# Second layer: separate SBUF places for the mixer weights of the second tile, and one load of each query weight for both tiles

## Chip, core and metric

The kernel runs on one core of a Trainium2 chip, as one launch. The metric is the time of that launch on the device, in microseconds, as the median of several runs. All data are float32; matrix products that feed later selections are formed either in float32 or as three float32r products (a high and a low part).

## What is computed

256 tokens of width 1024 go through two layers, 128 tokens (one tile) at a time where the text says tile 0 and tile 1. The first layer (a mixer, cross attention to a memory, and a layer of retrieved experts) is untouched by the change. The second layer, cut to what matters:

```python
n1 = rmsnorm_2(h, norm1_g)
proj = n1 @ w_in                       # q, k, v, r, a_lr, su, sv, ga, gb
y_a = gla_branch(...);  y_b = sgu_branch(...)
merged = sigmoid(ga) * (y_a @ w_branch_a) + sigmoid(gb) * (y_b @ w_branch_b)
h = h + merged @ w_out
n2 = rmsnorm_2(h, norm2_g)
h = h + peer_2(n2, peer_wq, ...)       # q = n2 @ peer_wq; scores against two key sets;
                                       # top 16 of 16 x 16 per head, 8 heads: 128 of 16384 experts per token
                                       # out = sum over the 128 of gate * gelu(u[e] . n2) * v[e]
return rmsnorm_2(h, final_g)
```

## The kernel before

**Weights.** Every large weight lies in HBM as chunks of 128 x 2048 float32 (1024 KB) in `wall`, and each chunk is one DMA, issued on the SP queue by `chunk` (L400) or `keep` (L412). The second layer's chunks go to a ring of four places, `WP` (columns 8192 to 16384 of the tile `BIG`, in the profile `big_sb`). `ring_w2.take(use, done)` hands out the next place and gives back the event that frees it: the read of the chunk that had the place four loads ago. SP waits for that event, then issues, and everything behind it in SP's program waits too.

**Uses.** For tile t the mixer of the second layer has four `up` chunks, ("up", 2, t, half, n), two for each branch, and four `square` chunks, ("sq", 2, t, n), the output projection. TensorE reads them at L863 (`up`) and L880 (`square`). Then come eight query chunks, one per head, ("q", 2, t, h), read at L966; the scores of two heads at a time are L981. Tile 0 takes heads 0 to 7 in order. Heads 4 to 7 of tile 0 go to places of their own, `KQ` (columns 24576 to 32768, where tile 1's gates and the constants of the mixer lie; so `keep` waits until tile 1's merge `mix_v "mg", 2, 1, 1` is over), and tile 1 starts with these four, as its uses 0 to 3. Its uses 4 to 7 are heads 0 to 3, which SP loads again through the ring. SP's list for the second layer is thus: 16 projection chunks, 4 `up` and 4 `square` of tile 0, heads 0 and 1, the `up` chunks of tile 1 with heads 2 and 3 between them, 4 `square` of tile 1, kept heads 4 to 7, and heads 0 to 3 once more (in `weights2`, L487 on).

**Experts.** Tile 0's first product with `u` is done by gathering: 128 indirect DMAs (L2317, GpSimd's own queue), each bringing one row of 1024 to each token (512 KB), into eight slots `UB`, columns 0 to 8192 of `BIG`. Two of three are multiplied and summed on VectorE (L2092), the third on GpSimd (L2338) and ScalarE. A slot is refilled when the dot product eight steps earlier is done. For tile 1 the product is dense: all 16384 rows of `u`, as 128 chunks `ut` of 512 KB on SP's queue (L581), four slots, read by TensorE at L1002; ScalarE takes every fourth chunk's results through gelu. In the same stretch one-hot gate blocks are formed on VectorE and multiplied on TensorE (L1021). Last come the values `v`: 128 chunks on SP's queue, read at L1040 and L1054.

**Order.** Each engine has one program. It is made of strands (generators), each of which yields a number, its beat, ahead of each piece, and `in_turn` merges the strands by these beats when the program is built. The beats are no times on the chip; they only fix an order, for each engine by itself. What runs when is settled by semaphores. VectorE's order around the change: `experts(2)`, the dot products, has beats from 1276 in steps of 2, tile 1's norm has 1278 to 1281; so the dot products of gathers 0 and 2 stand ahead of the two halves of tile 1's norm product. GpSimd's order is that of its gathers with a multiplication after each third. SP's order is the one given above, with `ut` chunks 0 to 3 at beat 1250 and the later ones from 1290 on, each behind the dense product four chunks before.

Around the change: `weight` (which place and which semaphore belong to a use), `weights2` (SP's order), `rows` of the GpSimd program (the gathers of `u`).

Of the kernel before, what the change touches and what calls it, by code (L numbers as in the profile page):

```python
# [13 lines left out]
WR = 4  # L14
UR = 8
FD = 640
RAW_COLS = 512
DR = 4
# [209 lines left out]
def build(nc, a):  # L228
    with ExitStack() as ctx:
# [10 lines left out]
        BIG = sb("big_sb", [128, 32768])  # L240
# [41 lines left out]
        def small(n, *name):  # L282
            if name not in columns:
# [60 lines left out]
        SQUARE = {1: 34, 2: 78, "co": 42}  # L344
# [11 lines left out]
             "gla_p gla_a gla_v gla_g sgu_p sgu_a sgu_v sgu_g kv_p kv_a").split()]  # L356
        vec_in, ident_in, wsm_in, cst_in, row_in, subk2_in, sguw_in, gup_in, wlr_in, sgub_in = loads = [landing(n) for n in (
            "vec_in ident_in wsm_in cst_in row_in subk2_in sguw_in gup_in wlr_in sgub_in").split()]
        x_in, mem_in, w_in, kq_in, tq_in, sub_in, u_in, ut_in, v_in, low_in, out_in = slots = [
            [landing(f"{n}{i}") for i in range(k)] for n, k in (  # L360
                ("x_in", 2), ("mem_in", 2), ("w_in", WR), ("kq_in", 4), ("tq_in", 4), ("sub_in", 6), ("u_in", UR), ("ut_in", DR), ("v_in", 6), ("low_in", 6), ("out", 2))]

        ring_a, ring_b, ring_c, ring_m = Ring(banks[2:4]), Ring(banks[4:6]), Ring(banks[6:8]), Ring(banks[0:2])
        WP = [BIG[:, 8192 + 2048 * i:8192 + 2048 * (i + 1)] for i in range(WR)]
# [4 lines left out]
        second = lambda use: use[0] in ("in2", "kv") or (use[0] in ("up", "sq", "q") and use[1] == 2)  # L369

        KQ = [BIG[:, 24576 + 2048 * i:24576 + 2048 * (i + 1)] for i in range(4)]
        TQ = [BIG[:, o:o + 2048] for o in (29696, 20992, 16384, 18432)]
        kept = lambda use: use[0:2] == ("q", 2) and (use[2] == 0 and use[3] > 3 or use[2] == 1 and use[3] < 4)

        def weight(use):
            if use in (("q", 1, 0, 4), ("q", 1, 0, 5), ("q", 1, 0, 6), ("q", 1, 0, 7), ("q", 1, 1, 1), ("q", 1, 1, 2), ("q", 1, 1, 3)):
                return TQ[use[3] % 4], tq_in[use[3] % 4].at("q")
            if kept(use):
                return KQ[use[3] % 4], kq_in[use[3] % 4].at(use[1])
            ring = ring_w2 if second(use) else ring_w  # L380
            return ring.place(use), w_in[ring.index(use)].at(use)
# [10 lines left out]
        def sync_program(e):  # L392

            def chunk(use, i, done):

                ring = ring_w2 if second(use) else ring_w
                place, free = ring.take(use, done)
                for f in free:
                    e.wait_ge(*f)
                e.dma_start(place, a["wall"][i]).then_inc(*w_in[ring.index(use)].up(use))  # L400
# [86 lines left out]
            def weights2():  # L487
                for n in range(4):
                    yield 860 + 32 * n
                    e.wait_ge(*val_v.at("gl", 1, STEPS.index((79 + 16 * n, (0, 1)))))  # L490
                    chunk(("kv", n), 54 + n, (kv_p, "kv", n, 1))
                for n in range(16):
                    yield 1085 + 3.4 * n if n < 4 else (1097, 1102, 1113, 1119, 1126, 1133, 1139, 1146, 1154, 1159, 1165, 1171)[n - 4]
                    chunk(("in2", n), 58 + n, (split_v, "lo", ("in2", n)))
                def up(t, h, n):
                    chunk(("up", 2, t, h, n), UP[2, h] + n, (mix_p, "up", 2, t, h, n))

                def square(t, n):
                    chunk(("sq", 2, t, n), SQUARE[2] + n, (mix_p, "sq", 2, t, n))

                def query(t, h):
                    if t == 0 and h > 3:
                        keep(2, h, mix_v.at("mg", 2, 1, 1))
                    else:
                        chunk(("q", 2, t, h), PQ[2] + h % 4, (sel_p, "q", 2, t, h))

                for h, n, b in ((0, 0, 1176), (0, 1, 1182), (1, 0, 1187), (1, 1, 1193)):
                    yield b
                    up(0, h, n)
                for n in range(4):  # L510
                    yield (1204, 1207, 1211, 1215)[n]
                    square(0, n)
                yield 1220
                query(0, 0)
                query(0, 1)
                for n in range(2):
                    yield 1228 + 5 * n
                    up(1, 0, n)
                    query(0, 2 + n)
                for n in range(2):  # L520
                    yield 1238 + 2 * n
                    up(1, 1, n)
                for n in range(4):
                    yield 1245 + 3 * n
                    square(1, n)
                for t, h in [(0, h) for h in range(4, 8)] + [(1, h) for h in range(4, 8)]:
                    yield 1264 + 0.1 * h if t == 0 else 1306 + 4 * h
                    query(t, h)

            def rows():  # L530
                yield 119.5
# [1746 lines left out]
        def gpsimd_program(e):  # L2278
# [40 lines left out]
            def rows(l):  # L2319
                T, dt = T_GATHER[l]  # L2320
                for k in range(128):
                    yield T + dt * k
                    if k % 32 == 0:
                        e.wait_ge(*sel_v.at("ix", l, 0, k // 32))
                    if k == 0:
                        e.wait_ge(*proj_p.at("mm", ("mv", 3) if l == 1 else ("in2", 15)))
                    if k >= UR:
                        e.wait_ge(*(dot_a if pooled(k - UR) else dot_v).at("dot", l, k - UR))
                    gather(UB[k % UR], a[f"u{l}"], k).then_inc(*u_in[k % UR].up(l, k))
# [137 lines left out]
```

## Time and profile before

| | |
|---|---|
| median of 3 runs | 2080.87 us (2074.07 to 2081.56) |
| the profiled execution | 2079.94 us, its span 2078.2 us |
| mean granted TensorE clock | 0.976 |
| busy, share of the span | TensorE 92%, weight loads of TensorE 81%, VectorE 66%, ScalarE 43%, GpSimd 38% |
| DMA | 627.08 MB, mean 302 GB/s |
| SP's queue (q1), software queue (q0), share of 16 DMA engines | 51.9%, 27.6% |
| weight loads on SP's queue | 123 issues into `big_sb`, 1024 KB each |

A row of a timeline gives the start and the length of a group of like instructions, the engine, the line, the operation with its tiles, how many they are, and in brackets the idle time of the engine before it with what ended it. SPq is the issuing of DMAs by SP, not their transfer. In the table by stage each row gives a stretch, its length, busy time of each engine with its instructions, the granted clock of TensorE, the busy share of the 16 DMA engines and what they moved. In rows on waits stand the total, how often, and the longest.

### The profile page before, as it was taken

The page shows a single profiled execution, that of the slowest core. Times are in us where ns is not written, and L with a number is a line of the kernel's source. Part 1 is how long each engine was busy: PE and PEld are TensorE (multiplying, and loading weights), DVE is VectorE, ACT ScalarE, POOL GpSimd, SP SyncE. Part 2 cuts the span into 40 slices and gives each one's busy share as a digit, 9 for nine tenths or more (in the row PEclk, how much of TensorE's full clock was granted, in tenths as well). Part 3 has the DMA queues.
Part 4 walks back from the last instruction along what each step waited for, and adds up shares of the span by engine and source line. Part 5 has one row for each costly group of instructions (what it writes and reads, how often), then busy time and mean ns, then how long its engine had stood idle before and what let it go on. Part 6 is the DMA issues. An engine that isn't in the chain of part 4 may idle for free.

```text
span 2078.2 us, 32948 instructions
## 1 busy us (share of the span) xinstructions
PE 1908.6 (92%) x12722; PEld 1673.2 (81%) x12722; DVE 1374.9 (66%) x2722; ACT 900.7 (43%) x1946; POOL 780.3 (38%) x626
## 2 busy tenths in 40 slices
PE   6999999987888999999999999887798899899998
PEld 6999988877888989676666889877798799767775
DVE  6643431378989948587775333268588798688884
ACT  5555443123236747444442553113223577544442
POOL 0000000068686635344431000047577744444441
PEclk9999999998999999999999999999999999999999
DMA  5433453899999988999995433699999978799996
GB/s 230 160 127 121 148 214 128 338 357 359 375 405 399 372 303 281 339 386 404 398 382 204 162 122 123 209 388 410 379 399 383 410 295 264 293 379 391 391 389 253
DMA packets 154874, 627.08 MB, mean 302 GB/s; under 512 B 19271, under 2 KB 22983, under 8 KB 138846
## 3 DMA queue, kind: packets, MB, share of 16 engines
q1 hardware_dynamic: 97374, 406.84, 51.9%
q0 software_dynamic: 57344, 218.14, 27.6%
q8 instruction: 101, 1.65, 0.3%
q14 instruction: 55, 0.45, 0.1%
HBM read 623.85 MB, written 1.05 MB: 301 GB/s over the span
## 4 chain that ended last, share of the span: by engine, by line
PE 35%; DMA 7%; issue 4%; DVE 2%; ACT 2%; POOL 0%; SPq 0%; DVEq 0%; POOLq 0%
PE bank L1002 7%; PE bank L1040 7%; PE bank L1054 5%; DMA ut_sb<-in_ut_dram 5%; PE bank_n L1054 4%; PE bank L966 3%; PE bank L1021 2%; PE bank L1085 1%; DMA big_sb<-in_u_dram,idx_sb 1%; PE bank L620 1%; PE bank L621 1%; PE bank L622 1%; DMA nt_sb<-in_v_dram 1%; PE bank L863 1%; DMA ab_sb<-in_v_dram 1%
## 5 line engine op out<-in xcount | busy, mean ns | idle before, releaser
L1002 PE MATMUL bank<-nt_sb,ut_sb 128*128 128x128 f32 x4096 | 508.4, 281 | 62.2 <-DMA ut_sb<-in_ut_dram 58.9
L1002 PEld LDWEIGHTS bank<-nt_sb,ut_sb 128*128 128x128 f32 x4096 | 486.2, 196 | 74.1 <-DMA ut_sb<-in_ut_dram 59.3
L2317 POOL DMA_INDIRECT big_sb<-in_u_dram,idx_sb x256 | 255.3, 997 | 243.7 <-ACT big_sb L1166 116.9
L1166 ACT ACTIVATE big_sb<-bank 128x512 f32<-128x512 f32 (+13 forms) x284 | 131.9, 477 | 352.5 <-PE bank L1002 127.7
L2281 POOL TENSOR_TENSOR sm_sb<-sm_sb,vec_sb 128x1 f32<-128x1 f32 (+2 forms) x24 | 19.5, 813 | 640.2 <-DVE sm_sb L1671 634.6
L2092 DVE CUSTOM_DVE_ANT_0 big_sb<-big_sb,bank_n 128x1024 f32<-128x1024 f32 x170 | 205.5, 1211 | 70.4 <-DMA big_sb<-in_u_dram,idx_sb 69.4
L2338 POOL TENSOR_TENSOR big_sb<-big_sb,nt_sb 128x1024 f32<-128x1024 f32 x86 | 205.0, 2385 | 11.2 <-DMA big_sb<-in_u_dram,idx_sb 8.4
L620 PE MATMUL bank<-n_hi,w_hi 128*128 128x256 f32 x608 | 181.5, 299 | 13.2 <-DVE w_lo L1668 13.1
L1166 ACT ACTIVATE big_sb<-big_sb 128x1024 f32<-128x1024 f32 (+2 forms) x132 | 116.5, 885 | 166.2 <-POOL big_sb L2338 152.7
L1054 PE MATMUL bank_n<-v_hi,g_hi 128*128 128x384 f32 x240 | 178.2, 743 | 0.0
L2317 POOL DMA_INDIRECT cst_sb<-in_vl_dram,idx_sb x102 | 124.2, 1218 | 142.3 <-DVE x_sb L1674 139.6
L621 PE MATMUL bank<-n_hi,w_lo 128*128 128x256 f32 x608 | 176.2, 290 | 0.0
L622 PE MATMUL bank<-n_lo,w_hi 128*128 128x256 f32 x608 | 175.9, 289 | 0.0
L1668 DVE TENSOR_TENSOR g_lo<-big_sb,g_hi 128x256 fp32r<-128x256 f32 x240 | 104.9, 437 | 107.1 <-ACT g_hi L1166 105.1
L2317 POOL DMA_INDIRECT spare_sb<-in_vl_dram,idx_sb x102 | 109.2, 1070 | 134.5 <-DVE x_sb L1674 124.2
L1668 DVE TENSOR_TENSOR w_lo<-big_sb,w_hi 128x2048 fp32r<-128x2048 f32 x46 | 105.2, 2289 | 68.9 <-ACT w_hi L1166 68.9
L620 PEld LDWEIGHTS bank<-n_hi,w_hi 128*128 128x128 f32 x608 | 120.8, 199 | 19.0 <-issue 16.8
L1166 ACT ACTIVATE v_hi<-nt_sb 128x512 fp32r<-128x512 f32 x120 | 75.8, 632 | 138.7 <-issue 85.9
L1040 PE MATMUL bank<-nt_sb,big_sb 128*128 128x512 f32 x260 | 132.9, 592 | 2.7 <-DMA nt_sb<-in_v_dram 2.7
L966 PE MATMUL bank<-nt_sb,big_sb 128*128 128x128 f32 x1024 | 121.9, 280 | 1.5 <-DMA big_sb<-in_wall_dram 0.8
L966 PEld LDWEIGHTS bank<-nt_sb,big_sb 128*128 128x128 f32 x1024 | 119.9, 197 | 2.3 <-issue 2.2
L621 PEld LDWEIGHTS bank<-n_hi,w_lo 128*128 128x128 f32 x608 | 121.1, 199 | 0.5 <-issue 0.5
(270 smaller groups left out, 4070.6 us busy)
## 6 DMA issues: line engine op xcount, KB each, us to landing
ut_sb<-in_ut_dram SPq DMA_DIRECT2D x256, 512.0 KB
big_sb<-in_wall_dram SPq DMA_DIRECT2D x123, 1024.0 KB, 10.8
nt_sb<-in_v_dram SPq DMA_DIRECT2D x130, 512.0 KB
sw_sb<-in_v_dram SPq DMA_DIRECT2D x84, 512.0 KB
ab_sb<-in_v_dram SPq DMA_DIRECT2D x42, 512.0 KB
big_sb<-in_u_dram,idx_sb POOLq DMA_INDIRECT x256
cst_sb<-in_vl_dram,idx_sb POOLq DMA_INDIRECT x102
spare_sb<-in_vl_dram,idx_sb POOLq DMA_INDIRECT x102
```

The lines of the kernel that those rows point to most:

```text
L620: e.matmul(out, lh(k), rh(k), start=k == 0, stop=False)
L621: e.matmul(out, ll(k), rh(k), start=False, stop=False)
L622: i = e.matmul(out, lh(k), rl(k), start=False, stop=k == 7)
L966: i = e.matmul(hs(bk, 2 * (h % 2) + c), w[:, k * 256 + c * 128:k * 256 + (c + 1) * 128], TN[t][:, k, :], start=k == 0, stop=k == 7)
L1002: i = e.matmul(hs(bk, c % 4), UT[:, c % DR, k * 128:(k + 1) * 128], TN[1][:, k, :], start=k == 0, stop=k == 7)
L1040: i = e.matmul(total[1][0], GM[:, 1, c, :], VSL[vslot(s)][:, 0:RAW_COLS], start=s == 0, stop=s == LAST[1])
L1054: i = e.matmul(total[1][1] if t else total[0], x[:, w, :], y[:, b, (0 if t else FD - RAW_COLS):], start=part == 0 and s == 0, stop=False)
L1166: return e.activation(out, in_, func, bias=bias, scale=scale, **kw)
L1668: return e.tensor_tensor(out, x, y, op)
L2092: e.tensor_tensor_reduce(g, g, NP[:, :], 1.0, 0.0, ALU.mult, ALU.add, H[:, k:k + 1]).then_inc(*dot_v.up("dot", l, k))
L2317: return e.indirect_dma_start(out, None, table, bass.IndirectOffsetOnAxis(ap=IDX[:, k:k + 1], axis=0))
L2338: e.tensor_tensor(UB[k % UR], UB[k % UR], N[:, 0, :], ALU.mult).then_inc(*dot_g.up("dot", l, k))
```

## The change

Tile 1's eight mixer chunks of the second layer get places `MQ` outside the ring, with semaphores `mq_in`: the `up` chunks in columns 0 to 8192 of `BIG` (the later gather slots), the `square` chunks in columns 0 to 4096 and 18432 to 22528. SP issues the four `up` loads directly behind query heads 0 and 1, after a wait for the last projection product; the first two `square` loads wait for tile 1's first two `up` products, the last two for both branch outputs of tile 1. Heads 0 to 3 of the query weights stay in the four ring places for both tiles: tile 1's uses 4 to 7 read the places of tile 0's uses 0 to 3, and the second load of these heads is gone. Gathers 0 and 2 of the second layer wait for tile 1's first and second `square` product, since their slots lie where those chunks are.

```diff
--- before.py
+++ after.py
@@ -356,9 +356,9 @@
              "gla_p gla_a gla_v gla_g sgu_p sgu_a sgu_v sgu_g kv_p kv_a").split()]
         vec_in, ident_in, wsm_in, cst_in, row_in, subk2_in, sguw_in, gup_in, wlr_in, sgub_in = loads = [landing(n) for n in (
             "vec_in ident_in wsm_in cst_in row_in subk2_in sguw_in gup_in wlr_in sgub_in").split()]
-        x_in, mem_in, w_in, kq_in, tq_in, sub_in, u_in, ut_in, v_in, low_in, out_in = slots = [
+        x_in, mem_in, w_in, kq_in, mq_in, tq_in, sub_in, u_in, ut_in, v_in, low_in, out_in = slots = [
             [landing(f"{n}{i}") for i in range(k)] for n, k in (
-                ("x_in", 2), ("mem_in", 2), ("w_in", WR), ("kq_in", 4), ("tq_in", 4), ("sub_in", 6), ("u_in", UR), ("ut_in", DR), ("v_in", 6), ("low_in", 6), ("out", 2))]
+                ("x_in", 2), ("mem_in", 2), ("w_in", WR), ("kq_in", 4), ("mq_in", 4), ("tq_in", 4), ("sub_in", 6), ("u_in", UR), ("ut_in", DR), ("v_in", 6), ("low_in", 6), ("out", 2))]
 
         ring_a, ring_b, ring_c, ring_m = Ring(banks[2:4]), Ring(banks[4:6]), Ring(banks[6:8]), Ring(banks[0:2])
         WP = [BIG[:, 8192 + 2048 * i:8192 + 2048 * (i + 1)] for i in range(WR)]
@@ -369,12 +369,18 @@
         second = lambda use: use[0] in ("in2", "kv") or (use[0] in ("up", "sq", "q") and use[1] == 2)
 
         KQ = [BIG[:, 24576 + 2048 * i:24576 + 2048 * (i + 1)] for i in range(4)]
+        MQ = [BIG[:, o:o + 2048] for o in (0, 2048, 4096, 6144, 0, 2048, 18432, 20480)]
         TQ = [BIG[:, o:o + 2048] for o in (29696, 20992, 16384, 18432)]
         kept = lambda use: use[0:2] == ("q", 2) and (use[2] == 0 and use[3] > 3 or use[2] == 1 and use[3] < 4)
 
         def weight(use):
             if use in (("q", 1, 0, 4), ("q", 1, 0, 5), ("q", 1, 0, 6), ("q", 1, 0, 7), ("q", 1, 1, 1), ("q", 1, 1, 2), ("q", 1, 1, 3)):
                 return TQ[use[3] % 4], tq_in[use[3] % 4].at("q")
+            if use[0:3] in (("up", 2, 1), ("sq", 2, 1)):
+                n = 2 * use[3] + use[4] if use[0] == "up" else use[3]
+                return MQ[n + 4 * (use[0] == "sq")], mq_in[n].at(use[0])
+            if use[0:3] == ("q", 2, 1) and use[3] > 3:
+                use = ("q", 2, 0, use[3] - 4)
             if kept(use):
                 return KQ[use[3] % 4], kq_in[use[3] % 4].at(use[1])
             ring = ring_w2 if second(use) else ring_w
@@ -499,10 +505,10 @@
                     chunk(("sq", 2, t, n), SQUARE[2] + n, (mix_p, "sq", 2, t, n))
 
                 def query(t, h):
-                    if t == 0 and h > 3:
+                    if h > 3:
                         keep(2, h, mix_v.at("mg", 2, 1, 1))
                     else:
-                        chunk(("q", 2, t, h), PQ[2] + h % 4, (sel_p, "q", 2, t, h))
+                        chunk(("q", 2, t, h), PQ[2] + h, (sel_p, "q", 2, 1, h + 4))
 
                 for h, n, b in ((0, 0, 1176), (0, 1, 1182), (1, 0, 1187), (1, 1, 1193)):
                     yield b
@@ -513,19 +519,24 @@
                 yield 1220
                 query(0, 0)
                 query(0, 1)
-                for n in range(2):
-                    yield 1228 + 5 * n
-                    up(1, 0, n)
-                    query(0, 2 + n)
-                for n in range(2):
-                    yield 1238 + 2 * n
-                    up(1, 1, n)
+                e.wait_ge(*proj_p.at("mm", ("in2", 15)))
+                for n in range(4):
+                    yield 1220.5 + 0.5 * n
+                    e.dma_start(MQ[n], a["wall"][UP[2, n // 2] + n % 2]).then_inc(*mq_in[n].up("up"))
+                for h in range(2, 4):
+                    yield 1225 + h
+                    query(0, h)
                 for n in range(4):
                     yield 1245 + 3 * n
-                    square(1, n)
-                for t, h in [(0, h) for h in range(4, 8)] + [(1, h) for h in range(4, 8)]:
-                    yield 1264 + 0.1 * h if t == 0 else 1306 + 4 * h
-                    query(t, h)
+                    if n < 2:
+                        e.wait_ge(*mix_p.at("up", 2, 1, 0, n))
+                    elif n == 2:
+                        e.wait_ge(*gla_v.at(1, "ya"))
+                        e.wait_ge(*sgu_v.at(1, "yb"))
+                    e.dma_start(MQ[4 + n], a["wall"][SQUARE[2] + n]).then_inc(*mq_in[n].up("sq"))
+                for h in range(4, 8):
+                    yield 1264 + 0.1 * h
+                    query(0, h)
 
             def rows():
                 yield 119.5
@@ -2324,6 +2335,8 @@
                         e.wait_ge(*sel_v.at("ix", l, 0, k // 32))
                     if k == 0:
                         e.wait_ge(*proj_p.at("mm", ("mv", 3) if l == 1 else ("in2", 15)))
+                    if l == 2 and k in (0, 2):
+                        e.wait_ge(*mix_p.at("sq", 2, 1, k // 2))
                     if k >= UR:
                         e.wait_ge(*(dot_a if pooled(k - UR) else dot_v).at("dot", l, k - UR))
                     gather(UB[k % UR], a[f"u{l}"], k).then_inc(*u_in[k % UR].up(l, k))
```

## Rows read from the trace of the kernel before

**Rows 1.** The page's 40 slices of 52 us, busy tenths of the DMA engines

```profile
DMA  5433453899999988999995433699999978799996
```

**Rows 2.** Table by stage: stretch, length, busy times, PEclk, DMA share, GB/s

```profile
1330.00:1350.00 20.00, 19.27 (x154) 19.11 (x154) 4.49 (x25) 2.51 (x4) 0.00 (x0) 0.90 0.35 115
1350.00:1365.00 15.00, 13.44 (x117) 13.20 (x116) 8.41 (x40) 1.17 (x5) 0.00 (x0) 1.00 0.97 376
...
1440.00:1475.00 35.00, 18.95 (x127) 17.70 (x127) 21.53 (x60) 8.37 (x16) 16.63 (x12) 0.89 1.02 413
1475.00:1480.00 5.00, 5.00 (x36) 5.00 (x36) 2.00 (x7) 1.64 (x3) 0.53 (x1) 0.75 0.66 239
...
1640.00:1685.00 45.00, 43.13 (x371) 42.11 (x372) 44.73 (x67) 35.93 (x116) 28.05 (x23) 1.00 1.01 393
1685.00:1790.00 105.00, 101.24 (x895) 100.23 (x895) 86.45 (x100) 81.19 (x245) 45.97 (x28) 1.00 0.71 239
```

**Rows 3.** Waits of TensorE, 1398 to 1690

```profile
PE bank L1002 <- DMA ut_sb<-in_ut_dram: 38.6, 31, 4.3
```

**Rows 4.** DMA view, 1350 to 1690: total, queues, issues

```profile
DMA packets 34569, 133.46 MB, mean 393 GB/s; under 512 B 3827, under 2 KB 3827, under 8 KB 32768
...
q0 software_dynamic: 18319, 66.74, 50.4%
q1 hardware_dynamic: 16221, 66.33, 49.2%
...
big_sb<-in_wall_dram SPq DMA_DIRECT2D x12, 1024.0 KB, 22.2
```

**Rows 5.** Timeline of SP's queue at 1437

```profile
1437.18 0.43 SPq L400 DMA_DIRECT2D big_sb<-in_wall_dram  x1
```

**Rows 6.** Timeline of TensorE at 1500

```profile
1500.51 3.74 PE L966 MATMUL bank<-nt_sb,big_sb 128*128 128x128 f32 x32
```

**Rows 7.** Waits of TensorE, 1437 to 1480

```profile
PE bank L1002 <- DMA ut_sb<-in_ut_dram: 16.1, 6, 4.3
```

**Rows 8.** Timelines of ScalarE and GpSimd, 1455 to 1490

```profile
1477.57 0.60 ACT L1166 ACTIVATE big_sb<-bank 128x512 f32<-128x512 f32 x1 [16.50 <-PE bank L1002]
...
1479.47 0.94 POOL L2317 DMA_INDIRECT big_sb<-in_u_dram,idx_sb  x1 [12.74 <-ACT big_sb L1166]
```

**Rows 9.** Timeline of SP's queue, 1320 to 1366

```profile
1320.47 19.11 SPq L400 DMA_DIRECT2D big_sb<-in_wall_dram  x4
...
1348.26 3.90 SPq L400 DMA_DIRECT2D big_sb<-in_wall_dram  x3
...
1364.01 1.75 SPq L412 DMA_DIRECT2D big_sb<-in_wall_dram  x4
```

**Rows 10.** Timeline of TensorE, 1309 to 1390

```profile
1309.84 14.05 PE L880 MATMUL bank<-big_sb,nt_sb 128*128 128x256 f32 x64 [1.55 <-DVE nt_sb L1668]
...
1343.60 3.74 PE L966 MATMUL bank<-nt_sb,big_sb 128*128 128x128 f32 x32
...
1364.08 1.10 PE L880 MATMUL bank<-big_sb,nt_sb 128*128 128x256 f32 x4 [1.56 <-DVE nt_sb L1668]
...
1387.66 2.15 PE L627 MATMUL bank<-cst_sb,nt_sb 128*128 128x128 f32 x8 [8.63 <-DVE nt_sb L1674]
```

**Rows 11.** Timelines of GpSimd and VectorE, 1369 to 1388

```profile
1369.20 1.02 POOL L2317 DMA_INDIRECT big_sb<-in_u_dram,idx_sb  x1 [42.95 <-DVE sv_sb L2079]
...
1371.78 0.94 POOL L2317 DMA_INDIRECT big_sb<-in_u_dram,idx_sb  x1 [0.30 <-issue]
...
1380.94 0.57 POOL L2281 TENSOR_TENSOR sm_sb<-sm_sb,vec_sb 128x1 f32<-128x1 f32 x1 [4.49 <-DVE sm_sb L1671]
...
1385.42 1.22 DVE L2092 CUSTOM_DVE_ANT_0 big_sb<-big_sb,bank_n 128x1024 f32<-128x1024 f32 x1 [4.36 <-DMA big_sb<-in_u_dram,idx_sb]
```

**Rows 12.** Groups by line, VectorE, 1350 to 1690: busy, mean ns, idle before

```profile
L2092 DVE CUSTOM_DVE_ANT_0 big_sb<-big_sb,bank_n 128x1024 f32<-128x1024 f32 x82 | 99.2, 1212 | 53.6 <-DMA big_sb<-in_u_dram,idx_sb 53.1 <-issue 0.3
```

**Rows 13.** Timeline of TensorE at the start of the last stage

```profile
1795.63 2.04 PE L1040 MATMUL bank<-sw_sb,big_sb 128*128 128x512 f32 x2 [5.08 <-issue]
```

## The prediction

> **What bounds the kernel now.** I began with the page's slices, to see where a change of weight loads can matter. From the 27th slice on (about 1350 us) the DMA row stands at 9 for six slices [rows 1]. The table by stage is sharper: from 1330 to 1350 the DMA engines are 0.35 busy, from 1350 to 1685 they are full (0.97 to 1.02 in its rows, up to 413 GB/s), and in 1685 to 1790 they are 0.71 busy while TensorE runs 101.2 of 105 us [rows 2]. The waits of TensorE agree: in 1398 to 1690 the dense matmuls (L1002) wait 38.6 us in 31 pieces, all for `ut` tiles [rows 3]. So stage A (1350 to 1685) is bound by bytes. It moves 133.5 MB at 393 GB/s, half on SP's queue and half on the software queue, with 12 weight loads among them [rows 4]. Behind it TensorE runs its fixed program to the end, so whatever stage A saves should reach the end, unless VectorE, 44.7 of 45 us busy in 1640 to 1685 [rows 2], holds it back.
>
> **Part 1: four loads disappear.** Before, heads 0 to 3 of the query weights are loaded a second time for tile 1, 1024 KB each, between the `ut` loads; the first of these four issues, at 1437.18, stands in [rows 5], the last comes at about 1454. Nobody is near needing them: the first query matmuls of tile 1 start at 1500.51, and these are its last four heads [rows 6]. They are 4 x 1.049 = 4.19 MB in a stretch whose engines are full at 413 GB/s [rows 2], so they cost 10.2 us of DMA time. What they do is plain in the same stretch: TensorE waits 16.1 us for `ut` in six pieces between 1437 and 1480 [rows 7]; ScalarE stands 16.50 us behind the dense group that is not finished, and since ScalarE also releases gather slots, GpSimd issues no gather for 12.74 us, up to 1479.47 [rows 8], after which the DMA share falls to 0.66 for 5 us [rows 2]. Their issues take 0.43 us each on SP [rows 5] and hold nobody. Gain: 10.2 us by bytes.
>
> **Part 2: loads that come earlier.** Before, tile 1's mixer weights go through four ring places, each waiting until a place is read out. Heads 0 and 1 are issued by about 1317; then come four loads from 1320.47 within 19.11 us, three from 1348.26 within 3.90 us, three more and four `ut` behind them, and the four kept query loads from 1364.01 [rows 9]. After, tile 1's four `up` loads leave right behind head 1, at about 1317.5 to 1319: their wait, for the last projection, is over before tile 0's mixer even begins, and tile 0's last mixer product starts at 1309.84 [rows 10]. Heads 2 and 3 keep their times, about 1320.5 and 1324. The first two `square` loads wait for tile 1's first two `up` products, which free ring places at 1348.3 and about 1351.8 as now; `ut` follows, and the last two `square` loads leave at about 1354. The kept heads wait for the merge, 1364.0, as before. So two loads (2.10 MB) that stood at 1348.3 now run in the idle 1320 to 1350. At 410 GB/s stage A begins with 5.1 us less queued. What that is worth can be seen: the third gather is issued at 1371.78 and its data are taken at 1385.42, 13.6 us later. The product of tile 1's norm stands behind it on VectorE, though its factor was ready at 1380.94 + 0.57 = 1381.5 [rows 11], and TensorE idles 8.63 us, until 1387.66 [rows 10]. A third gather that lands by 1381.5 takes 1385.42 + 1.2 - 1381.5 = 5.1 us out. Late next is the norm's own chain.
>
> **Part 3: the waits it adds.** Gather 0 waits for the first `square` product of tile 1, gather 2 for the second. The `square` matmuls begin at 1364.08, and the 64 of tile 0 took 14.05 us [rows 10], so the parts end at about 1367.6, 1371.2 and so on. Gather 0 is issued at 1369.20, when VectorE has its indices, gather 2 at 1371.78 [rows 11]. Slack 1.6 and 0.6 us: nothing is paid. If it were gone, every gather behind it on GpSimd would move with it. SP's new waits (branch outputs, `up` products) are for events of before 1352. The four loads put in front of heads 2 and 3 cost these at most their own bytes: 4.2 MB, 10.2 us from 1324, and head 2 is read from 1343.60 [rows 10]. Head 1 goes ahead of them. Taken at zero. No work of TensorE, VectorE or ScalarE changes.
>
> **Sum.** 10.2 + 5.1 = 15.3 us of DMA time. How much of it reaches the end no row shows. The low end is 5 us (only the earlier start goes through, because VectorE is the limit in 1640 to 1685); the high end is 21 us: 15.3, the 1.7 us of empty DMA time in 1475 to 1480, and some 4 us of the pause of 12.74. I take 13.0, near the bytes, since the DMA engines are full for 335 us, less 2.3 us because VectorE is also close to full at the stage's end. 2079.9 (the profiled execution, span 2078.2) - 13.0 = 2066.9; the median of the three runs is 0.9 above that execution. I predict **2067**; this case alone would hold 2063 to 2071.
>
> On the size of part 1 the Trainium skill speaks too: in "DMA: Bandwidth & Descriptors", Specifications, it gives about 358 GB/s as the share of HBM for one core; by that the four loads would be worth 11.7 us. The trace has 413 GB/s in that stretch [rows 2], so the measurement decides.
>
> **Rivals.** (a) *Only the earlier start survives.* Gathers do not profit from the missing weight loads: they come on another queue, which in 1350 to 1690 has 50.4% of the DMA time against 49.2% [rows 4]. Then `ut` comes sooner, but VectorE, which takes gathers and gate blocks in one order, is where it was but for part 2. Gain about 5 to 7 us, 2074. For it: VectorE 44.7 of 45 us. Against it: VectorE waits 53.1 us for gathers in stage A [rows 12], so it has room. By the Trainium skill ("DMA: Bandwidth & Descriptors", Queues, rings and completion order) each DMA engine takes packets in turn from the queues that have work; by that rule a fuller SP queue does not take the gathers' turn, which is this rival. The near equal shares agree. 0.19.
>
> (b) *Hidden anyway.* The bytes are saved but TensorE's 38.6 us of waits only move, for instance to the later score products; 2080. The full DMA engines speak against it. 0.08.
>
> (c) *More than the bytes.* The pause of 12.74 us goes whole and the empty DMA time behind it too, on top of the earlier start: 5.1 + 12.7 + 1.7 = 19.5; 2060. It decides if the gathers, not the bytes, set the pace there. 0.12.
>
> (d) *Slower: the lockstep pause comes back at worse places.* ScalarE's one queue holds both the gelu of dense groups and the release of gathers; where a dense group is late, GpSimd stands, as at 1466. The new phase between the `ut` stream and the gathers is given by nobody. If a pause of 12.74 us comes at two other places, 25.5 - 13 = 12 us more than now: 2092. It decides from two pauses of over 10 us on. Against it: the cause of this one, weights in front of `ut`, is removed. 0.07.
>
> **Numbers.** Forecast 0.54, (a) 0.19, (b) 0.08, (c) 0.12, (d) 0.07. About 0.5% (10.4 us) is what a measurement can tell from no change, so faster is the forecast and (c), 0.66; within is (a) and (b), 0.27; slower 0.07. The range 2057 to 2077 takes in (c), the forecast and (a).
>
> **What would show it.** Weight loads 4 fewer and 4.19 MB less on SP's queue. Four loads directly behind 1317. Gather 2 read by about 1381 and tile 1's transposes at about 1382.5 instead of 1387.66. First gather still near 1369.2: if it is later, part 3 is wrong. TensorE's waits for `ut` in stage A down from 38.6 by some 10 us, and no pause near 1466. First matmul of the final stage (L1040, 1795.6 now [rows 13]) at about 1782.5; its 262 us unchanged. If L1040 moves by 5 only, (a) holds and VectorE shows no waits for gathers before 1680.

## The result, and the profile after

The changed kernel takes 2066.89 us (median, 2060.85 to 2070.33), the kernel before 2081.13 us beside it (2073.78 to 2082.45): a ratio of 0.9933, 95% interval 0.991 to 0.9956. 2067 was forecast, in a range of 2057 to 2077. The number came out right. The experiments show that the terms behind it did not: one is worth nothing that they can measure, one is larger than it was put.

| | before | after |
|---|---|---|
| profiled execution, its span | 2079.94, 2078.2 us | 2062.73, 2060.9 us |
| mean granted clock | 0.976 | 0.978 |
| DMA | 627.08 MB | 622.89 MB |
| 1024 KB loads into `big_sb` | 123 | 119 |

After's span is 17.3 us shorter, but 9.2 us of that is there already at the head of the experts' stage: matmul 8701 of the program (of 12722), about 1378 us before, starts 9.2 us earlier, matmul 8001, at 1270 us and ahead of everything that is changed, already 6.4 us earlier. The same kernel before, profiled once more, was 8.8 us early at matmul 8701 too (6.1 at 8001), and the changed kernel once more 1.2 us. This is scatter between executions, and a comparison of two profiles has to leave it out. Positions below are therefore compared by an event inside each trace, or with the lead of 9.2 us added ("on the old clock").

The part that the change moved earlier, on SP's queue of the changed kernel (a line of a timeline: start, length, engine, line, operation, count):

```profile
1305.66 3.78 SPq L406 DMA_DIRECT2D big_sb<-in_wall_dram  x2
1309.49 2.14 SPq L525 DMA_DIRECT2D big_sb<-in_wall_dram  x4
1312.57 3.78 SPq L406 DMA_DIRECT2D big_sb<-in_wall_dram  x2
1339.06 3.90 SPq L536 DMA_DIRECT2D big_sb<-in_wall_dram  x2
1343.01 2.15 SPq L592 DMA_DIRECT2D ut_sb<-in_ut_dram  x4
1345.26 0.91 SPq L536 DMA_DIRECT2D big_sb<-in_wall_dram  x2
1354.81 2.20 SPq L418 DMA_DIRECT2D big_sb<-in_wall_dram  x4
```

The four `up` loads (L525) leave behind heads 0 and 1 as the diff says, where [rows 9] had them at places that came free one by one. Next come GpSimd's first gathers and the small product of tile 1's norm, then VectorE's dot products and the halves of the norm product:

```profile
1360.01 1.02 POOL L2328 DMA_INDIRECT big_sb<-in_u_dram,idx_sb  x1 [41.67 <-DVE sv_sb L2090]
1362.58 0.94 POOL L2328 DMA_INDIRECT big_sb<-in_u_dram,idx_sb  x1 [0.30 <-issue]
1371.75 0.57 POOL L2292 TENSOR_TENSOR sm_sb<-sm_sb,vec_sb 128x1 f32<-128x1 f32 x1 [4.50 <-DVE sm_sb L1682]
...
1374.76 2.36 POOL L2351 TENSOR_TENSOR big_sb<-big_sb,nt_sb 128x1024 f32<-128x1024 f32 x1
```

```profile
1368.83 1.22 DVE L2103 CUSTOM_DVE_ANT_0 big_sb<-big_sb,bank_n 128x1024 f32<-128x1024 f32 x1 [6.08 <-DMA big_sb<-in_u_dram,idx_sb]
...
1372.54 1.22 DVE L2103 CUSTOM_DVE_ANT_0 big_sb<-big_sb,bank_n 128x1024 f32<-128x1024 f32 x1 [0.66 <-DMA big_sb<-in_u_dram,idx_sb]
...
1373.90 0.73 DVE L1685 SCALAR_TENSOR_TENSOR nt_sb<-x_sb,sm_sb,row_sb 128x512 f32<-128x512 f32 x1
...
1374.95 2.72 DVE L1685 SCALAR_TENSOR_TENSOR nt_sb<-x_sb,sm_sb,row_sb 128x512 f32<-128x512 f32 x1
```

Gather 0 goes at 1360.01, which is 1369.2 on the clock of [rows 11] once the lead of 9.2 us is added, and what ended its wait is VectorE's indices, as before: the new wait costs nothing. Gather 2's data (issued at 1362.58) are taken at 1372.54, after a wait of 0.66 us in place of 4.36. But the second half of the norm product takes 2.72 us where its twin takes 0.73: it begins while GpSimd's product of 2.36 us (1374.76 to 1377.12) runs, and ends 0.55 us behind it. TensorE gets the halves one after the other:

```profile
1374.78 1.09 PE L638 MATMUL bank<-cst_sb,nt_sb 128*128 128x128 f32 x4 [4.95 <-DVE nt_sb L1685]
...
1377.82 1.09 PE L638 MATMUL bank<-cst_sb,nt_sb 128*128 128x128 f32 x4 [1.96 <-DVE nt_sb L1685]
```

With the lead added the first half comes at 1384.0, against 1387.66 before [rows 10], and the second at 1387.0, against 1388.72 (the eight matmuls of 1387.66 are two groups of four, and the second begins 1.06 us behind the first): 3.7 and 1.7 us earlier.

The table by stage of the changed kernel (columns as in [rows 2]), beside which [rows 2] stands:

```profile
1330.00:1350.00 20.00, 19.27 (x173) 19.27 (x173) 7.46 (x40) 1.88 (x2) 0.00 (x0) 1.00 0.47 173
...
1365.00:1390.00 25.00, 18.10 (x118) 16.84 (x117) 19.74 (x66) 4.66 (x9) 17.87 (x15) 0.80 0.88 324
1390.00:1440.00 50.00, 43.72 (x364) 42.50 (x363) 42.53 (x112) 15.97 (x34) 38.37 (x30) 0.97 1.01 398
1440.00:1475.00 35.00, 28.30 (x226) 25.91 (x224) 22.11 (x78) 12.70 (x22) 27.93 (x23) 1.00 1.03 408
1475.00:1480.00 5.00, 4.61 (x41) 4.61 (x42) 4.55 (x8) 1.36 (x3) 4.53 (x3) 1.00 1.04 412
...
1640.00:1685.00 45.00, 41.16 (x346) 40.24 (x345) 45.00 (x61) 32.88 (x108) 22.40 (x15) 0.96 0.77 279
```

Read 1440 to 1475: the DMA engines are as full as before and move as much (408 against 413 GB/s), but TensorE works 28.3 us in place of 18.95 and GpSimd 27.9 in place of 16.6, and the hole at 1475 to 1480 (share 0.66) is gone. The stretches are cut by each trace's own clock, so this row lies 9.2 us further on in the work than its fellow; the second profile of the changed kernel, with a lead of 1.2 us only, has the same row:

```profile
1440.00:1475.00 35.00, 27.98 (x224) 25.61 (x222) 23.96 (x70) 13.34 (x24) 28.04 (x22) 1.00 1.03 409
```

In 1365 to 1390, which is 5 to 30 us behind the first gather, there is a new hole: share 0.88. Before, the same 25 us of the work have no hole:

```profile
1374.20:1399.20 25.00, 16.37 (x106) 15.13 (x105) 16.06 (x53) 4.59 (x9) 17.43 (x15) 0.80 1.00 396
```

TensorE's and GpSimd's waits in the stage, and the DMA view of 1350 to 1690:

```profile
PE bank L1013 <- DMA ut_sb<-in_ut_dram: 24.0, 36, 2.2
```

```profile
POOL big_sb L2328 <- ACT big_sb L1177: 46.4, 24, 5.9
```

```profile
DMA packets 34085, 127.52 MB, mean 375 GB/s; under 512 B 3792, under 2 KB 3792, under 8 KB 33287
...
q0 software_dynamic: 18432, 67.12, 50.7%
q1 hardware_dynamic: 15623, 60.00, 45.1%
...
big_sb<-in_wall_dram SPq DMA_DIRECT2D x4, 1024.0 KB, 6.4
```

The waits for `ut` fall from 38.6 to 24.0 us, the longest from 4.3 to 2.2; the pause of GpSimd behind ScalarE, 12.74 us [rows 8], has no successor over 5.9; the four weight loads left in this window land 6.4 us after their issue, where the twelve of before took 22.2 [rows 4].

### The profile page after: what moved, and what is told of

The parts are those of the page before. It is cut to its first block and busy times, and to the rows that moved or that the text cites. A ratio compares the mean times of both kernels' runs of the same rounds, so it can differ in the third digit from the quotient of the medians.

```text
span 2060.9 us, 32945 instructions
## 1 busy us (share of the span) xinstructions
PE 1905.3 (92%) x12722; PEld 1670.1 (81%) x12722; DVE 1369.8 (66%) x2722; ACT 900.9 (44%) x1946; POOL 773.6 (38%) x626
## 2 busy tenths in 40 slices
DMA packets 154298, 622.89 MB, mean 302 GB/s; under 512 B 19207, under 2 KB 22919, under 8 KB 138782
```

## The experiments

All were timed in five rounds beside the kernel before; ratios are to it, and 0.001 is 2.1 us. Three numbers of each profile go beside the ratio. *Stage*: from the issue of the second layer's first gather to the start of its last (85th) dot product on VectorE. *Stretch*: from the 9101st to the 9401st matmul (1439.5 to 1500.5 before). *Pause*: the longest wait of GpSimd's gathers for ScalarE in 1390 to 1690.

| kernel | ratio, 95% interval | stage | stretch | pause |
|---|---|---|---|---|
| before (as profiled first) | | 329.1 | 61.0 | 12.7 |
| again_before | 1.0009, 0.9997 to 1.0021 | 336.2 | 62.8 | 11.3 |
| e_reload | 1.0001, 0.9989 to 1.0014 | 331.4 | 60.4 | 10.8 |
| k_bunch | 0.9998, 0.9982 to 1.0013 | 330.2 | 60.4 | 17.1 |
| f_pool | 0.9997, 0.9985 to 1.0009 | 329.3 | 53.5 | 5.9 |
| f_spread | 0.9993, 0.9977 to 1.0008 | 329.4 | 53.3 | 8.9 |
| k_pieces | 0.9987, 0.997 to 1.0004 | 331.5 | 56.0 | 8.5 |
| f_half | 0.9973, 0.9954 to 0.9992 | 328.2 | 53.9 | 6.8 |
| after (as profiled first) | 0.9933, 0.991 to 0.9956 | 320.0 | 46.1 | 5.9 |
| again_after | 0.9938, 0.9921 to 0.9956 | 317.9 | 46.7 | 5.5 |
| e_late | 0.9941, 0.9924 to 0.9957 | 320.5 | 47.5 | 5.7 |
| h_trade | 0.9962, 0.9946 to 0.9977 | 322.2 | 54.1 | 8.9 |
| g_utless | 0.9922, 0.99 to 0.9944 | 317.4 | 45.9 | 6.8 |
| g_local | 0.9901, 0.9879 to 0.9922 | 313.4 | 42.6 | 5.5 |

**Which part brings the gain.** again_before and again_after are the two kernels as they are. e_reload is the changed kernel with the second load of heads 0 to 3 put back, at the beats of before, into the places where the same data lie: part 2 without part 1.

```diff
+                for h in range(4):
+                    yield 1322 + 4 * h
+                    e.wait_ge(*sel_p.at("q", 2, 0, h))
+                    e.dma_start(ring_w2.place(("q", 2, 0, h)), a["wall"][PQ[2] + h]).then_inc(
+                        *w_in[ring_w2.index(("q", 2, 0, h))].up("q", 2, 1, h + 4))
```

e_late is the changed kernel with SP's old order and old waits for the mixer chunks of tile 1: part 1 without the early issue.

```diff
-                for n in range(4):
-                    yield 1220.5 + 0.5 * n
-                    e.dma_start(MQ[n], a["wall"][UP[2, n // 2] + n % 2]).then_inc(*mq_in[n].up("up"))
-                for h in range(2, 4):
-                    yield 1225 + h
-                    query(0, h)
...
+                for n in range(2):
+                    yield 1228 + 5 * n
+                    own(n, (sel_p.at("q", 2, 0, 0) if n else mix_p.at("sq", 2, 0, 2)))
+                    e.wait_ge(*(sel_p.at("q", 2, 0, 1) if n else mix_p.at("sq", 2, 0, 3)))
+                    query(0, 2 + n)
...
```

> The unchanged kernel once more, as the measure of what a repeated build and a repeated execution give. All theories: ratio to the kernel before 1.000, interval including 1. In the two profiled executions so far the changed kernel was already 6.4 us ahead when the second layer's projections ran, before any instruction that the change touches. If that lead is chance between executions, this one may show a shift of some us at the same point too (either sign); if it belongs to the changed kernel, this one stands within 1 us of the first trace up to there.

> The changed kernel once more. All theories: 2067 plus or minus 3 us, ratio 0.993. If the lead of 6.4 us ahead of the change was chance, it differs here by some us; the gain between tile 0's last mixer product of the second layer and the last stage stays at about 10 to 12 us in either case.

> Part 2 alone: the new places and the early loads, but heads 0 to 3 are loaded a second time for tile 1, into the place where they already lie, at the same places in SP's order as before. My theory (bytes in the full stage): part 1 is worth 10.2 us, so this gains only some 4 us over the kernel before, ratio 0.998, and TensorE waits again 16 us for ut near 1440 to 1480 with a pause of the gathers of over 10 us. Rival (the early start carries the gain): ratio 0.995 or less. Rival (the second load is hidden anyway): same as the changed kernel, 0.993.

> Part 1 alone: heads 0 to 3 are loaded once, tile 1's mixer weights have their own places, but each of their loads waits for the same event as before and stands at the same place in SP's order. My theory: it gains the 10 us of the four loads and lacks at most the 5 us of the earlier start; the trace of the changed kernel showed only about 2 us from that start, so I expect ratio 0.994 to 0.996. Rival (early start carries the gain): 0.998 or more. Gathers still begin when VectorE has the indices.

Measured: 2083.93, 2068.65, 2084.12 and 2069.97 us. With the reloads back nothing is left of the gain (e_reload's ratio is 0.0008 under again_before's, and the two intervals overlap), where 4 us were expected; with the old order all of it stays. Part 2 is worth nothing that can be measured (by the lower end of e_reload's interval at most 0.0011, 2.3 us; e_late against the two ratios of the changed kernel gives 0.6 to 1.7 us for it, with some 5 on each side), and part 1 is the gain. The traces show where part 2 goes. Start of the second layer's dot products on VectorE, counted from the first gather's issue:

| | dot product 2 | 3 | 9 | 13 | 17 |
|---|---|---|---|---|---|
| before | 16.2 | 19.6 | 40.4 | 48.7 | 63.8 |
| again_before | 16.4 | 19.7 | 40.0 | 48.3 | 63.4 |
| e_late | 16.6 | 19.9 | 40.3 | 48.6 | 63.7 |
| e_reload | 13.0 | 18.9 | 40.2 | 48.4 | 63.5 |
| after | 12.5 | 17.9 | 37.7 | 46.4 | 61.7 |
| again_after | 12.7 | 17.9 | 37.8 | 48.0 | 63.3 |

The second dot product is 3.2 to 4.1 us earlier in the three kernels whose mixer loads are early. At the third, half or more is gone, since VectorE has lost 1.9 to 2.6 us beside GpSimd's product; in e_reload the half product took 3.29 us. Some 50 us later nothing is left in e_reload and again_after and 2 us in the changed kernel's first profile. The reloads are not the reason in e_reload: the first of them is issued 67.5 us behind the first gather, after all of this table. There it is the first half of the norm product that meets GpSimd's product, in the changed kernel the second; that half starts 14.36 us behind the first gather in e_reload, 13.89 and 14.07 in the two profiles of the changed kernel, and GpSimd's product between 14.74 and 14.84 in all three, so less than half a microsecond decides which it is. The cleanest pair for part 1 is therefore e_late against the kernel before, whose dot products stand within 0.4 us of each other up to here. From the 8701st to the 9101st matmul all six kernels need 60.9 to 62.3 us. So an early DMA at the head of the stage met an engine that could not use it; in 1390 to 1440 VectorE is 42.5 to 46 of 50 us busy in all of them. That VectorE, in its fixed order, is what binds there is inferred from this and was not tried by itself.

**What the reloads cost, and by what.** The expectation for part 1 was 10.2 us; the stretch is 13 to 17 us shorter without the reloads (46.1 to 47.5 against 60.4 to 62.8). The pause near 1466 could be a cost of its own, caused by four weight loads within 25 us ahead of the dense chunks. Five kernels bring the reloads back in other ways. f_spread issues one per ten chunks of the dense weights:

```diff
-                    yield 1322 + 4 * h
+                    yield 1322 + 24 * h
```

> The kernel with the four reloads (2084.1 us) once more, but the four 1024 KB loads are issued one per ten chunks of the dense weights (about one each 24 us from 1440 us on) instead of one per one or two chunks. Theory A, bytes alone (4.19 MB at the 408 to 417 GB/s of the full slices cost 10.2 us wherever they lie in the full stage): the spread changes nothing, 2084, and each of the four later stretches is longer by 2.6 us. Theory B, bytes plus a knock-on of their coming together (dense weights late, TensorE late, ScalarE behind, gather places not released, a pause of the gathers of 12 to 14 us near 1466 us): the pause is gone and only the bytes are paid, about 2079 to 2080, 4 us below the bunched kernel and some 10 us above the kernel without reloads. Theory C, only the knock-on counts and the bytes are hidden: 2070.

f_half reloads two heads only (`for h in range(2)`); it takes 2076.72 us.

> The kernel with the reloads, but only heads 0 and 1 are loaded again (2.10 MB instead of 4.19 MB), heads 2 and 3 are read from where they lie. Theory A, bytes alone, linear: half of the 14.5 us between the kernel with four and that with none, so 2076 to 2077, or 2074 if 10.2 us is the whole price. Theory B, bytes plus a knock-on from the bunch: 5.1 us for the bytes, and the pause near 1466 us is under 7 us or absent: 2074 to 2075. Theory C, only a pause counts that needs all four: 2070.

f_pool has the four loads in the GpSimd program, with semaphores of their own:

```diff
+            def again():
+                for h in range(4):
+                    yield 1332.5 + 4 * h
+                    e.wait_ge(*sel_p.at("q", 2, 0, h))
+                    e.dma_start(ring_w2.place(("q", 2, 0, h)), a["wall"][PQ[2] + h]).then_inc(*ag_in[h].up("q"))
```

> The kernel with the four reloads, at about the same time, but issued from GpSimd's queue between the gathers, so that they no longer stand ahead of the dense weights in SyncE's queue. Theory A, bytes: 2084, whichever queue carries them. Theory B, what costs beyond 10.2 us is that the dense weights stand behind the reloads on one queue: the waits of TensorE for ut_sb fall and the stretch from 1440 to 1500 us is 3 to 5 us shorter, 2080, unless the gathers behind them on GpSimd's queue are late in place of them, which would show as a gap of the gathers and 2084 or more.

k_pieces has eight loads of `[:, 1024 * j:1024 * (j + 1)]` of a chunk, at beats `1322 + 12 * n`; k_bunch issues the four at one beat, 1328.

> The kernel with the four reloads (2084 us), each cut into two loads of 512 KB (half of every row of a tile of weights), one such load per five chunks of the dense weights, over the same time as the spread one (2080 us). Theory A, what a reload costs beyond 8 us (the price of eight dense loads of the same bytes in this stretch) is that 1024 KB stand at once ahead of a dense chunk that TensorE needs next: in pieces of the dense loads' own size it costs 8 us or less, 2076 to 2077. Theory B, the size of the piece does not matter, only that the loads are spread: 2080 as with whole loads. Theory C, spreading brings nothing and 2080 was scatter: 2083 to 2084.

> The kernel with the four reloads, all four issued one right behind the other on SyncE's queue with no dense chunk between them, where they were one per one or two chunks. Theory A, coming together costs by itself (spread they cost some 10.5 us, two chunks apart 13 to 14.5): 2086 to 2090, with a longer wait of TensorE for ut_sb, 8 us or more in one, and a gap of the gathers of over 14 us. Theory B, only the bytes in this stretch count: 2083 to 2084. Theory C, one long stall is absorbed better than four: 2080 or less.

k_bunch is the sharpest of these. Its SP timeline (L544 the reloads, L598 `ut`), and the waits of TensorE (L1019 the dense products) and of GpSimd (L2334 the gathers):

```profile
1442.04 1.86 SPq L544 DMA_DIRECT2D big_sb<-in_wall_dram  x4
1443.94 8.36 SPq L598 DMA_DIRECT2D ut_sb<-in_ut_dram  x4
```

```profile
PE bank L1019 <- DMA ut_sb<-in_ut_dram: 38.4, 38, 15.0
```

```profile
POOL big_sb L2334 <- ACT big_sb L1183: 62.6, 36, 17.1
```

TensorE waits 15.0 us at once and GpSimd 17.1, both as theory A said and longer than in any other kernel, and the time is 2082.41 us, a ratio of 0.9998 against the 1.0001 of e_reload: what A said of the time is refuted, and B holds within the interval. f_pool has no wait of TensorE over 1.9 us and no pause over 5.9, and takes 2080.89. f_spread takes 2078.97, k_pieces 2081.05. Theory B's 2079 to 2080 for f_spread and 2080 for f_pool stand near these medians, but their intervals take in 1.000, and the traces speak against a saving: in f_spread and k_pieces the stretch is 4 to 7 us shorter than in e_reload and the stage as long within 2 us (329.4 and 331.5 against 331.4): by these two profiles they pay later. The mean over the seven profiles with four reloads is a stage of 331.0 us (329.1 to 336.2), over the three without 319.5 (317.9 to 320.5): 11.5 us, or 10.7 if again_before's 336.2, which stands apart from the other six (329.1 to 331.5), is left out. By the times, the mean ratio of the six timed with reloads is 0.99975 and of the three without 0.99373, so 0.0060 of 2083 or 12.5 us. f_half gets back 0.0025 of these 0.0060 (its interval allows 0.0006 to 0.0044): some four tenths, where its bytes are half. Queue, moment, size of the piece and bunching do not matter within what these runs tell apart, some 2 to 3 us; the bytes do.

**What the same bytes are worth elsewhere.** g_utless and g_local are the changed kernel without eight of the 128 `ut` loads, the same 4.19 MB, and TensorE multiplies with the chunk that lies in the place; h_trade is e_reload without the eight of g_local. The tuple shown is that of g_local and h_trade; in g_utless it is `range(12, 108, 12)`.

```diff
+LEFT_OUT = (20, 21, 26, 27, 32, 33, 38, 39)
...
+                    if l == 2 and c in LEFT_OUT:
+                        continue
                     e.dma_start(UT[:, c % DR, :], a[f"ut{l}"][4 * dense_place(l, c // 4) + c % 4]).then_inc(*ut_in[c % DR].up(l, c))
```

> The changed kernel (2068.7 us) less eight of the 128 loads of 512 KB of the second layer's dense weights, every twelfth from the 13th to the 97th: 4.19 MB less, the same sum as the four query loads, spread over the stage. The kernel leaves out those loads and multiplies with the chunk that lies in the place, all other work as it is. Theory A, the stage is bound by bytes: 10.2 us at 410 GB/s, 2058 to 2059. Theory B, bytes plus lateness of the dense weights for TensorE: as much or a little more, 2055 to 2058. Rival: after the change another engine bounds (VectorE 97% busy at times), so the bytes bring clearly less than before: 2064 or more.

> The kernel with the four reloads (2084.1 us) less eight loads of 512 KB of the dense weights in the same stretch (chunks 20, 21, 26, 27, 32, 33, 38, 39; the chunk that lies in the place is multiplied in their stead), so that its bytes are those of the changed kernel. Theory A, bytes of either kind have one price, and the four reloads cost 14.5 us because of their 4.19 MB: 2069 to 2071. Theory B, a reload costs by what it is (1024 KB ahead of the dense weights on SyncE's queue, all within 25 us) and the eight dense loads are worth only what leaving them out of the changed kernel is worth, 2 to 4 us: 2080 to 2082.

> The changed kernel (2068.7 us) less the same eight dense loads, all between 1440 and 1510 us, where the reloads stood. Theory A, up to the changed kernel the bytes bind in this stretch, and behind it VectorE and the chain of its gathers do (the eight loads spread over the stage brought 2 to 4 us): 2065 to 2067. Theory B, the bytes still bind in this stretch, and only the later part of the stage has another bound: the stretch of 46 us is 6 to 10 us shorter, 2059 to 2062. Theory C, the gathers give the freed time back: 2069.

g_utless takes 2064.23 us, g_local 2061.88, h_trade 2075.66. By the ratios the eight loads in the reloads' stretch are worth 7.7 us behind the change (0.9938 to 0.9901) and 8.1 with the reloads present (1.0001 to 0.9962): one price on both sides as far as these ratios tell, whose intervals leave some 6 and 4 us on each side (by the stages it is 6 us behind the change and 9 with the reloads present). The gain of g_local is itself clear, so the change did not go past a point where the bytes stop to count there. The price is under 10.2 by some 2 us, less than the intervals leave. g_local's time is what its theory B said, but the stretch is only 3.5 to 4.1 us shorter (42.6), not 6 to 10. Its rows show some of the rest as DMA engines that are no longer full in 1475 to 1500 (a share of 0.94, where the changed kernel has 1.03):

```profile
1440.00:1475.00 35.00, 29.78 (x251) 28.28 (x250) 27.92 (x83) 12.28 (x22) 29.71 (x23) 1.00 1.00 387
1475.00:1500.00 25.00, 25.00 (x227) 25.00 (x226) 17.22 (x46) 6.77 (x13) 19.30 (x16) 1.00 0.94 360
```

Spread over the stage they are worth 3.3 us (0.9938 to 0.9922, the intervals overlap), though the DMA share of g_utless from its first gather to its last dot product is 0.97. I expected 10.2 from bytes alone; theory A failed for g_utless, and its rival (2064 or more) came. Whether 3.3 and 7.7 differ the ratios do not tell (their intervals are 0.99 to 0.9944 and 0.9879 to 0.9922); that 3.3 is under 10.2 they do. A reason was not found. One of its eight loads falls before 1440, where part 2 was lost too, and one behind 1640, where VectorE is full (45.00 of 45 us), but that leaves six. The busy share of the DMA engines was thus no measure here of what a byte is worth.

h_trade missed both A (2069 to 2071) and B (2080 to 2082): taking out eight `ut` loads makes up for some six tenths of the reloads, not for all. Whether 12 against 8 us is a difference of kind or scatter stays open; the intervals leave 2 to 3 us on each side of the 12 and 4 to 6 of the 8.

## Why the prediction was right, step by step

- **The bound.** "Stage A is bound by bytes" holds where the reloads stood (11 to 13 us for the 4.19 MB of the reloads, some 8 for as many bytes of `ut`), but not for the whole of 1350 to 1685 as the prediction took it: at its head (part 2) saved bytes bring nothing, spread over it 3 us, with an interval of several us.
- **Part 1, 10.2 us by bytes.** The right mechanism, somewhat under-sized: 10.7 to 11.5 us by the stages, 12.5 by the times. Given the scatter, 10.2 lies at the low edge of what was measured.
- **Part 2, 5.1 us.** This step is wrong: 0, by e_reload, and at most 2.3. Its first part came true: gather 2's data were taken 3.7 us sooner (on the old clock at 1381.7, after a wait of 0.66 in place of 4.36 us). That is already less than 5.1: the prediction's subtraction counts the dot product as over by 1381.5, so the data had to be there by 1380.3, where its text asks for 1381.5 only. "Late next is the norm's own chain" was the gap. The norm product now meets GpSimd's product and loses 2 us, the tile's halves come 3.7 and 1.7 us earlier, and 50 us later 0 to 2 us are left of what VectorE had gained. The DMA share of 0.88 in 1365 to 1390, against 1.00 in the same part of the work before, shows some 3 us of it given back as empty DMA time (0.12 of 25 us).
- **Part 3, zero.** Right: gather 0 at 1369.2 on the old clock, released by VectorE as before.
- **Less 2.3 us for VectorE.** No run tests it alone. VectorE is 45.00 of 45 us busy in 1640 to 1685, 44.73 before [rows 2], which says that it is full there and not what that costs. Sum: 15.3 - 2.3 = 13.0 was forecast, taken off a profiled execution that lay 1.2 us under the median of 2081.13, which makes 14 us from there; 11.5 + 0 or 12.5 + 0 is what the runs show, and 14.2 is the difference of the two medians. A term too many by 5.1, one too small by 1 to 2 and a discount that no run shows agree by chance, and the forecast of 2067 is no evidence for its reasons.
- **Rival (a), only the earlier start survives**, is refuted, and reversed: nothing of it survives that can be measured. **(b)** is refuted by the 0.0060. **(c), the pause goes whole on top**: the pause did go (5.9 us is the longest), but it is a place where the lost time appears and not a cost beside the bytes: k_bunch has one of 17.1 and no later end, f_pool none over 5.9 and no earlier end that its interval shows. The prediction read 12.74 us there as a further prize of 4 us at the high end; it was none. **(d)** did not come.
- **The signs that it named.** Four loads and 4.19 MB less: yes. Loads behind the first two: yes. Transposes at 1382.5 instead of 1387.66: 1384.0 for the first half on the old clock, 1387.0 for the second (1388.72 before), so mostly no. Waits for `ut` down by some 10: by 14.6. The last stage begins at 1779.20, not at about 1782.5:

```profile
1779.20 2.04 PE L1051 MATMUL bank<-sw_sb,big_sb 128*128 128x512 f32 x2 [6.87 <-issue]
```

That is 16.4 us earlier, of which 9.2 is the chance lead; 7.2 is what this one pair of profiles shows, less than the medians do. From here to the span's end it is 281.7 us, before 282.6; the prediction wrote 262 for this, which was a slip in the subtraction and entered no sum.

## What to carry to other kernels

A load that is made twice cost its bytes here, where the DMA engines are full and another engine waits for them, wherever in that stretch, on whichever of the two queues and in whatever pieces it was issued, within 2 to 3 us; drop it rather than move it. A long stall in a profile is not a prize of its own: ask whether the time is merely collected there, and test it by making the stall worse. Before adding the gain of an earlier transfer, follow the engine that takes it for 50 us on, and take both profiles of a pair from an event inside the traces, since 9 us of a difference of 17 here was chance.

## What the hardware showed unasked

A VectorE product of two SBUF tensors (128x512) takes 0.73 us alone and waits GpSimd's product out when the two meet: 2.72 us in the changed kernel, 2.61 in again_after, 3.29 in e_reload. In the 14 traces 11 such halves overlap a GpSimd product; they take 2.61 to 3.57 us, and each ends 0.56 us behind it (0.55 by the rounded figures of the rows shown). None of the others takes over 0.79. In e_reload the half product starts at 1385.72 and ends at 1389.01, GpSimd's product runs 1386.10 to 1388.46, so the ends lie 0.55 us apart, as in the changed kernel. By these rows VectorE's product began first, by 0.38 us (in k_pieces by 0.66), and still it ended last; spans of GpSimd are rough, so which of the two was first stays open:

```profile
1385.72 3.29 DVE L1691 SCALAR_TENSOR_TENSOR nt_sb<-x_sb,sm_sb,row_sb 128x512 f32<-128x512 f32 x1
```

```profile
1386.10 2.36 POOL L2357 TENSOR_TENSOR big_sb<-big_sb,nt_sb 128x1024 f32<-128x1024 f32 x1
```

A small copy does the same: 128x64 in 1.98 us before, beside GpSimd's product of 1396.43 to 1398.79, and 0.17 us after, when none runs:

```profile
1396.88 1.98 DVE L2033 CAST sv_sb<-su_sb 128x64 f32<-128x64 uint32 x1
```

```profile
1386.30 0.17 DVE L2044 CAST sv_sb<-su_sb 128x64 f32<-128x64 uint32 x1
```

The dot products, which read one operand from a PSUM bank, do not: the one at 1381.07 in the changed kernel takes 1.20 us beside a GpSimd product that starts at 1381.03, and of the 81 in this trace that overlap one none takes over 1.22.

```profile
1381.07 1.20 DVE L2103 CUSTOM_DVE_ANT_0 big_sb<-big_sb,bank_n 128x1024 f32<-128x1024 f32 x1
```

```profile
1381.03 2.36 POOL L2351 TENSOR_TENSOR big_sb<-big_sb,nt_sb 128x1024 f32<-128x1024 f32 x1
```

The Trainium skill has this rule ("SBUF — State Buffer", SBUF: two separate sides): the port pair that VectorE and GpSimd share is locked for a whole instruction, for a VectorE operation with two SBUF inputs among others. The traces agree for the product of two SBUF tensors, by the ends of the two products, 0.55 us apart in both kernels; the prediction did not weigh it where it moved VectorE's product towards GpSimd's.
